# The first eight units of a two-layer model on halves of unscaled x, with the norm's row applied at eviction

## The chip, the cores and the metric

The kernel runs on one core of a Trainium2 chip. The metric is the time of one execution on the device in microseconds (us). Times are given as the median of three runs.

## The reference

The reference is a whole model in float32: a block with a state-space mixer (SSD) and a diagonal recurrence (S5), and then two layers with convolution, windowed attention and a gated feed-forward part. Only its entrance matters here: 16 meta tokens are put ahead of 512 tokens of x, and the first projection is made of the normalised result.

```python
def _rmsnorm(x, g):
    xf = x.astype(jnp.float32)
    y = xf * lax.rsqrt(jnp.mean(xf * xf, axis=-1, keepdims=True) + NORM_EPS)
    return (y * g.astype(jnp.float32)).astype(x.dtype)
...
    h = jnp.concatenate([meta, x], axis=1)            # 528 tokens x 1024
...
        n = _rmsnorm(h, g_mix[layer])
        proj = n @ w_in[layer]
        z = proj[..., :o_xbc]
        xbc = jax.nn.silu(_causal_depthwise_conv(proj[..., o_xbc:o_dt], conv_w[layer], conv_b[layer]))
        dt_raw = proj[..., o_dt:o_u]
        u = proj[..., o_u:]
        y_ssd = _ssd_mixer(xbc, dt_raw, z, ...)       # uses softplus(dt_raw + dt_bias)
        y_s5 = _s5_mixer(u, lam_re, lam_im, ...)      # uses powers of exp((lam_re + i lam_im) * step)
```

The factor of the norm is one number for each token, so it can be multiplied to a token's column of the projection after the product instead of to the input before it. The gain g belongs to a row of the weights and can't.

## The kernel before, in words

**Units.** All weight products are cut into units: 128 output features by 1024 inputs, eight tiles (kt) of 128 by 128. Products are made of two reduced-precision halves: a weight tile w becomes whi and wlo = w - whi, the activation becomes xhi and xlo, and a bank receives whi*xhi + whi*xlo + wlo*xhi. For 528 tokens a product is two matmuls of 264 columns into two banks, so a unit is 8 x 3 x 2 = 48 matmuls. There are R = 4 slots, unit g uses slot g % 4, and slot s owns the banks 2s and 2s+1. The order of units in the projection is: 0 to 7 are u (the S5 input), 8 is dt, 9 to 20 are xbc, 21 to 28 are z.

**Who does what for a unit.** The SP queue loads the raw weights (`wraw`, L2795) as soon as GpSimd has finished with the slot. ScalarE makes the high half (`split_hi`, L257), after the unit that used the slot before is done. GpSimd makes the low half (`split_lo`, L265) after that. TensorE waits for the high half and for the slot's banks to be read (`pe_unit`, L304), does the high products, waits for the low half and does the rest. The engine that reads the banks raises `acc_free`.

**Order.** Each engine's program is a list written out by hand; there is no planner. An engine does its list strictly in order. Every producer has a semaphore with a step count (`Steps`). All 86 of them are raised by four rounds at the start (`credit`), so that waits never ask for a small value. GpSimd does this in a block of its own, `setup`, with 8 more increments for `unit_done` and `acc_free`, 94 in all, and every engine meets the others at that block's end before the first DMA is issued.

**The entrance.** SP loads x in four quarters (`xin`) and then the weights of units 0 to 3. ScalarE squares the eight tiles of x (L440), VectorE adds them (L451), TensorE sums over the partitions (L528), ScalarE takes the root, VectorE the reciprocal, TensorE spreads it over the partitions as a row (L536), ScalarE copies the row to `nrs` (L459). Then, for each kt, VectorE multiplies x by gain and row into `ntt` (L580), ScalarE rounds it to xhi (L488), VectorE subtracts to xlo (L590). TensorE warms up with `keep_busy` matmuls (L509) meanwhile, then does units 0 to 3 together as the halves arrive (`pe_quad`, L338), and from unit 4 on one after the other (L304).

**Behind it.** ScalarE reads the banks of u into `uk` (L657) with a store that scatters neighbouring tokens by 66 elements, and a DMA on ScalarE's queue writes `uk` out. After the norm VectorE computes the powers for S5 (`s5_powers_dve`, small instructions of L1207, each with a drain), which need two sines of ScalarE (`s5_sin_act`, L1228 and L1229). Only then it comes to dt: it makes `dty` (L709), ScalarE takes exp and ln of it (L669, L671), and only behind those in ScalarE's list come the reads of the banks of xbc (L682, L684), each followed by the split of the unit four further on. VectorE does three taps of the convolution for each xbc tile (L724).

## Time and profile before

| | us |
|---|---|
| median of three runs | 2898.86 |
| lowest and highest | 2894.07, 2901.11 |
| the profiled execution | 2893.15 |
| its span (first to last instruction) | 2891.3 |
| TensorE busy in it | 2807.3 |
| from the span's start to the first DMA issue | 8.42 |
| to the first matmul of unit 0 | 28.58 |

The profile is of one execution. Durations and starts are read from it, in microseconds from the span's start. PE is TensorE's matmul side and PEld its weight load, DVE is VectorE, ACT ScalarE, POOL GpSimd, SP SyncE; a q behind the name is the engine's queue. L338 is line 338 of the kernel.

### The profile page before, as it was taken

To read this page: it belongs to the slowest core of one execution; us is meant where nothing else is said; L and a number is where in the kernel's file an instruction comes from. 1 tells how busy PE (TensorE), PEld (TensorE's weight loads), DVE (VectorE), ACT (ScalarE), POOL (GpSimd) and SP (SyncE) were. 2 spreads that over 40 slices of the span, in tenths; PEclk is the share of its full clock that TensorE was granted. 3 is DMA by queue.
4 is the path that set the end of the run, shared out by engine and by line. 5 is a ranking of instruction groups with operands and counts; after the bars stand their busy time and mean duration, and the time that the engine had idled before them with its cause. 6 is when DMAs were issued, how large, how long until landed. Compare 5 with 4: busy or idle time off the path is not lost.

```text
span 2891.3 us, 41476 instructions
## 1 busy us (share of the span) xinstructions
PE 2807.3 (97%) x15810; PEld 2289.6 (79%) x15810; DVE 1499.8 (52%) x1960; ACT 1083.9 (37%) x1662; POOL 1304.4 (45%) x752
## 2 busy tenths in 40 slices
PE   7998998999999999999999999999999999999998
PEld 6985744878888878877787888888887778788887
DVE  6865595453323345368874532422455877452535
ACT  4435222333323223235543422322343554342433
POOL 3444223434444264278842322222347894344343
PEclk9999999999999999999999999999999999999999
DMA  4335498333232243432232212122233223233332
GB/s 176 97 103 196 155 300 260 116 95 102 81 108 87 89 130 126 152 99 88 70 95 59 74 59 73 58 66 59 66 102 117 88 66 92 76 102 95 95 100 74
DMA packets 109736, 306.90 MB, mean 106 GB/s; under 512 B 29008, under 2 KB 37328, under 8 KB 109072
## 3 DMA queue, kind: packets, MB, share of 16 engines
q1 hardware_dynamic: 87584, 284.49, 31.2%
q10 hardware_dynamic: 19648, 16.66, 2.0%
q0 software_dynamic: 2352, 3.67, 0.4%
q8 instruction: 102, 1.67, 0.2%
q14 instruction: 50, 0.41, 0.0%
HBM read 294.95 MB, written 7.45 MB: 105 GB/s over the span
## 4 chain that ended last, share of the span: by engine, by line
PE 86%; DVE 4%; DMA 2%; POOL 2%; issue 2%; ACT 1%; DVEq 1%; SPq 0%; ACTq 0%; POOLq 0%
PE ps L304 41%; PE ps L338 17%; PE ps L329 6%; PE ps L1951 3%; PE ps L1947 3%; PE ps L1952 3%; PE ps L1955 3%; POOL wlo L265 2%; PE ps L2364 2%; PE ps L752 1%; PE ps L2024 1%; PE ps L2005 1%; DMA wada<-w_ada 1%; DVE nacc L451 1%; PE ps L1993 1%
## 5 line engine op out<-in xcount | busy, mean ns | idle before, releaser
L265 POOL TENSOR_TENSOR wlo<-wraw,whi 128x1024 fp32r<-128x1024 f32 x373 | 924.2, 2488 | 1308.4 <-ACT whi L257 1306.0
L257 ACT ACTIVATE whi<-wraw 128x1024 fp32r<-128x1024 f32 x373 | 392.0, 1054 | 454.5 <-PE ps L304 170.5
L304 PE MATMUL ps<-xah,whi 128*128 128x512 f32 x992 | 387.9, 391 | 1.7 <-issue 1.7
L304 PE MATMUL ps<-xal,whi 128*128 128x512 f32 x992 | 387.4, 391 | 0.0
L304 PE MATMUL ps<-xah,wlo 128*128 128x512 f32 x992 | 280.1, 391 | 0.0
L2250 DVE SCALAR_TENSOR_TENSOR co<-ub,vec,co 128x512 f32<-128x512 f32 (+1 forms) x216 | 254.3, 1216 | 4.2
L304 PEld LDWEIGHTS ps<-xah,whi 128*128 128x128 f32 x992 | 186.1, 188 | 42.7 <-issue 2.7
L304 PEld LDWEIGHTS ps<-xal,whi 128*128 128x128 f32 x992 | 186.1, 188 | 40.3
L304 PEld LDWEIGHTS ps<-xah,wlo 128*128 128x128 f32 x992 | 186.1, 188 | 40.2
L2351 POOL TENSOR_TENSOR co<-co,ct 128x512 f32<-128x512 f32 (+1 forms) x144 | 165.7, 1150 | 21.4 <-issue 1.3
L304 PE MATMUL ps<-hhi,whi 128*128 128x512 f32 x408 | 159.3, 390 | 0.0
L304 PE MATMUL ps<-hlo,whi 128*128 128x512 f32 x408 | 158.8, 389 | 0.0
L1113 DVE SCALAR_TENSOR_TENSOR res<-ps,mod,res 128x512 f32<-128x512 f32 (+1 forms) x64 | 47.6, 748 | 201.8 <-PE ps L329 110.0
L2707 DVE SCALAR_TENSOR_TENSOR f<-ps,vec,f 128x511 f32<-128x511 f32 x88 | 50.1, 611 | 196.3 <-ACT f L2668 196.3
L2349 POOL TENSOR_TENSOR ct<-ub,vec 128x512 f32<-128x512 f32 (+1 forms) x144 | 138.0, 958 | 26.8 <-issue 16.6
L1951 PE MATMUL ps<-xah,whi 128*128 128x512 f32 x352 | 143.5, 408 | 4.2 <-DVE ub L2262 2.6
L1952 PE MATMUL ps<-xal,whi 128*128 128x512 f32 x352 | 137.7, 391 | 0.0
L2665 ACT ACTIVATE f<-ps,vec 128x512 f32<-128x512 f32 x44 | 34.3, 780 | 186.6 <-PE ps L329 179.2
L1111 DVE TENSOR_TENSOR res<-res,ps 128x512 f32<-128x512 f32 x48 | 33.0, 688 | 132.2 <-PE ps L304 70.2
L304 PE MATMUL ps<-hhi,wlo 128*128 128x512 f32 x408 | 100.9, 389 | 0.0
L329 PE MATMUL ps<-xchi,whi 128*128 128x256 f32 x352 | 99.5, 283 | 0.0
L329 PE MATMUL ps<-xchi,wlo 128*128 128x256 f32 x352 | 99.3, 282 | 0.0
(417 smaller groups left out, 6014.8 us busy)
## 6 DMA issues: line engine op xcount, KB each, us to landing
wraw<-stream SPq DMA_DIRECT2D x425, 512.0 KB, 3.5
wada<-w_ada SPq DMA_DIRECT2D x56, 512.0 KB, 10.3
wraw<-w_ada SPq DMA_DIRECT2D x40, 512.0 KB, 3.8
biasb<-attn_bias ACTq DMA_DIRECT2D x32, 256.0 KB, 3.3
xin<-x0T SPq DMA_DIRECT2D x4, 528.0 KB, 6.5
s_u<-uk ACTq DMA_DIRECT2D x8, 264.0 KB, 2.7
res<-x0T ACTq DMA_DIRECT2D x1, 2048.0 KB, 9.1
outT<-res SPq DMA_DIRECT2D x4, 512.0 KB, 2.6
```

The source lines that it names most:

```text
L257: act.activation(whi[:, s], wraw[:, s], ACT.Copy).then_inc(hi_done[s], 1)
L265: pool.tensor_tensor(wlo[:, s], wraw[:, s], whi[:, s].bitcast(F32), ALU.subtract).then_inc(lo_done[s], 1)
L304: last = pe.matmul(ps[:, bank, 0:b - a], w[:, s, kt], x[:, kt, c0 + a:c0 + b], start=start, stop=stop)
L329: return pe.matmul(ps[:, R + s, 0:CTX], w[:, s, kt], part[:, kt], start=start, stop=stop)
L338: last = pe.matmul(ps[:, bank, 0:b - a], w[:, s, kt], x[:, kt, c0 + a:c0 + b], start=start, stop=stop)
L1947: last = pe.matmul(o, wraw[:, s, kt], x1[:, kt, 0:p.T], start=kt == 0, stop=kt == NT - 1)
L1951: pe.matmul(o, whi[:, s, kt], xah[:, kt, 0:p.T], start=kt == 0, stop=False)
L1952: pe.matmul(o, whi[:, s, kt], xal[:, kt, 0:p.T], start=False, stop=False)
L1955: last = pe.matmul(o, wlo[:, s, kt], xah[:, kt, 0:p.T], start=False, stop=kt == NT - 1)
L2250: dve.scalar_tensor_tensor(o, ub[:, m, k:k + p.T], colr(f"dw{p.l}", 1, k * 4 + m), o, ALU.mult, ALU.add)
L2349: pool.tensor_tensor(ct[:, 0:T], ub[:, m, k:k + T], colr(f"dw{l}", 1, k * 4 + m).to_broadcast([P, T]), ALU.mult)
L2351: ins = pool.tensor_tensor(o, o, ct[:, 0:T], ALU.add)
```

## The change

The first eight units work on halves of x times gain without the norm's factor (`xrh`, `xrl`), which exist as soon as x is there. ScalarE makes the high halves of x, VectorE the low ones, both in between the squares and their sum. TensorE does units 0 to 2 side by side as the halves arrive (`pe_first`), with the low products of the weights three steps late and the norm's sums and rows in the middle; banks 6 and 7, slot 3, stay with the norm. Then come unit 3 and units 4 to 7 one after the other, on the same unscaled halves. VectorE reads their banks and multiplies by the row `nrs` on the way (`u_dve`), in place of ScalarE; ScalarE only issues the DMA. The scaled halves xhi and xlo are made as before, for unit 8 and later. The `setup` block is gone: GpSimd gives 5 of the credits and the 8 increments at the start of the one block, and the other 81 credits behind its first four low halves. SP loads x and the weights in turns. `keep_busy(pe, bank, n)` was called three times, with 6, 4 and 4; now it is called once, with 4. Buffers from SC on move up to a boundary of 512 bytes (SA); their renaming is left out below.

```diff
+    xrh = at("xrh", [P, NT, TM], SA, F32R)
+    xrl = at("xrl", [P, NT, TM], SA + XB, F32R)
+    NS = SA + 2 * XB
...
+    def pe_first(pe):
+        n = NORM["mix"]
+        late = 3
+        def product(j, w, x, kt, start=False, stop=False):
+            for bank, a, b in parts_of(j, TM, True):
+                last = pe.matmul(ps[:, bank, 0:b - a], w[:, j, kt], x[:, kt, a:b], start=start, stop=stop)
+            return last
+        for kt in range(NT + late):
+            if kt < NT:
+                pe.wait_ge(raw_hi, kt + 1)
+                for j in range(R - 1):
+                    if kt == 0:
+                        hi_split(pe, U_U + j, 0, 0)
+                        pe.wait_ge(acc_free[j], 1)
+                    product(j, whi, xrh, kt, start=kt == 0)
+                pe.wait_ge(raw_lo, kt + 1)
+                for j in range(R - 1):
+                    product(j, whi, xrl, kt)
+            if kt == 6:
+                norm_sums_pe(pe, n, TM)
+            if kt == NT + late - 3:
+                norm_rows_pe(pe, n, TM)
+            if kt >= late:
+                for j in range(R - 1):
+                    if kt == late:
+                        lo_split(pe, U_U + j, 0, 0)
+                    last = product(j, wlo, xrh, kt - late, stop=kt == NT + late - 1)
+                    if kt == NT + late - 1:
+                        last.then_inc(unit_done[j], 1)
+    def u_act(act, m):
+        act.wait_ge(acc_free[slot(U_U + m)[0]], read_out(U_U + m))
+        act.dma_start(ud[m], uk[:, m % 2].rearrange("p k c -> p (k c)")).then_inc(s_uw[m % 2], 16)
+    def u_dve(dve, m):
+        s, rnd = slot(U_U + m)
+        dve.wait_ge(unit_done[s], rnd + 2)
+        if m >= 2:
+            dve.wait_ge(s_uw[m % 2], 16 * (m // 2))
+        dve.tensor_tensor(uk[:, m % 2].rearrange("p k (a c) -> p a c k", a=2),
+                          ps[:, 2 * s:2 * s + 2, 0:HALF].rearrange("p a (c k) -> p a c k", k=LB),
+                          nrs[:, :].rearrange("p (a c k) -> p a c k", a=2, k=LB), ALU.mult).then_inc(acc_free[s], 1)
+    def mix_norm_act(act):
+        for kt in range(NT):
+            norm_hi_act(act, NORM["mix"], kt, TM)
+            if kt == 2:
+                u_act(act, 0)
+                u_act(act, 1)
+                split_hi(act, U_U + R)
+            elif kt == 5:
+                u_act(act, 2)
+                split_hi(act, U_U + R + 1)
+        u_act(act, 3)
+        for m in range(2, R):
+            split_hi(act, U_U + R + m)
+    def mix_also_dve(dve, kt):
+        if kt == 1:
+            u_dve(dve, 0)
+            u_dve(dve, 1)
+        elif kt == 4:
+            u_dve(dve, 2)
+        elif kt == 7:
+            u_dve(dve, 3)
     def proj_pe(pe):
...
-        pe_quad(pe, U_U, 0, 0, xhi, xlo, TM, wide=True, **normed("mix"))
-        loop_u(U_U + R, 1, TM)
+        pe_first(pe)
+        pe.wait_ge(n_root.sem, n_root.past("root", 1))
+        pe_unit(pe, U_U + R - 1, 0, 0, xrh, xrl, TM, wide=True)
+        loop(pe, 1, lambda i: [pe_unit(pe, U_U + R + j, i, 1, xrh, xrl, TM, wide=True) for j in range(4)])
...
     def proj_act(act):
-        for m in range(NT):
-            s, rnd = slot(U_U + m)
-            act.wait_ge(unit_done[s], rnd + 2)
-            if m >= 2:
-                act.wait_ge(s_uw[m % 2], 16 * (m // 2))
-            act.activation(uk[:, m % 2].rearrange("p k (a c) -> p a c k", a=2),
-                           ps[:, 2 * s:2 * s + 2, 0:HALF].rearrange("p a (c k) -> p a c k", k=LB), ACT.Copy).then_inc(acc_free[s], 1)
+        for m in range(R, NT):
             split_hi(act, U_U + m + R)
-            act.wait_ge(acc_free[s], read_out(U_U + m))
-            act.dma_start(ud[m], uk[:, m % 2].rearrange("p k c -> p (k c)")).then_inc(s_uw[m % 2], 16)
+            u_act(act, m)
...
+        unit(4)                              # s5_powers_dve, behind its small instructions
         dve.wait_ge(s_5b, 16)
...
-        cmul(dve, bbar[:, 0], bbar[:, 1], (bin5[:, 0], bin5[:, 1]), (wide(q(CR)), wide(q(CI))), ta, tb)
+        cmul(dve, bbar[:, 0], bbar[:, 1], (bin5[:, 0], bin5[:, 1]), (wide(q(CR)), wide(q(CI))), ta, tb, lambda: unit(5))
+        unit(6)
+        unit(7)
         powers(dve, pw)
...
-    with nc.Block() as setup:
-        @setup.gpsimd
-        def _(pool):
-            for s in every_steps:
-                s.credit(pool)
-            for s in range(R):
-                pool.nop().then_inc(unit_done[s], 1)
-                pool.nop().then_inc(acc_free[s], 1)
...
-            for g in range(R):
-                load(g, g)
+            load_x(0)
+            load(0, 0)
+            load(1, 1)
+            load_x(1)
+            load(2, 2)
+            load_x(2)
+            load_x(3)
+            load(3, 3)
...
-            keep_busy(pe, 5, 6)
-            norm_sums_pe(pe, NORM["mix"], TM)
-            keep_busy(pe, 5, 4)
-            norm_rows_pe(pe, NORM["mix"], TM)
-            keep_busy(pe, 5, 4)
+            keep_busy(pe, 7, 4)
...
+            def half(kt):                    # ScalarE
+                act.wait_ge(s_in[kt // 2], 16)
+                act.activation(xrh[:, kt], xin[:, kt], ACT.Copy, scale=colr("g_mix", 1, kt)).then_inc(raw_hi, 1)
...
+            half(0)
+            split_hi(act, 0)
+            half(1)
+            split_hi(act, 1)
+            split_hi(act, 2)
+            half(2)
+            for kt in range(3, NT):
+                square(kt - 3)
+                half(kt)
+            split_hi(act, 3)
+            for kt in range(NT - 3, NT):
+                square(kt)
             root_ahead(act)
...
             for kt in range(NT):             # VectorE
+                dve.wait_ge(raw_hi, kt + 1)
+                dve.scalar_tensor_tensor(xrl[:, kt], xin[:, kt], colr("g_mix", 1, kt), xrh[:, kt].bitcast(F32), ALU.mult, ALU.subtract).then_inc(raw_lo, 1)
+                if kt >= 2:
+                    norm_add(dve, NORM["mix"], kt - 2, TM)
+            for kt in range(NT - 2, NT):
                 norm_add(dve, NORM["mix"], kt, TM)
...
+            early = [e_pa, e_pv, n_acc, n_sq, n_sum]
+            for s in early:
+                s.credit(pool)
...
             for g in range(R):
                 split_lo(pool, g)
+            for s in every_steps:
+                if s not in early:
+                    s.credit(pool)
```

## Rows read from the trace of the kernel before

**Rows 1.** The page's first part, busy time and share of the span

```profile
PE 2807.3 (97%) x15810; PEld 2289.6 (79%) x15810; DVE 1499.8 (52%) x1960; ACT 1083.9 (37%) x1662; POOL 1304.4 (45%) x752
```

**Rows 2.** The chain that ended last, 0 to 160: start, us, what

```profile
33.46 24.38 PE ps L338 x186
57.84 102.20 PE ps L304 x829
```

**Rows 3.** SP's waits to 12, its first issue (start, us), and wraw's four first loads

```profile
SPq L2772 <- PEq L2772: 7.6, 1, 7.6
...
8.42 0.40 SPq L2784 DMA_DIRECT2D pm<-s_lam  x1
...
L2795 SPq DMA_DIRECT2D wraw<-stream x4: 447/485/554, 11.0 to 12.5; - x4
...
DMA to landing us min/median/max: 8.3/9.3/10.4
```

**Rows 4.** ScalarE and VectorE by time, 81 to 141: start, us, instruction, [idle before]

```profile
81.23 1.19 ACT L657 ACTIVATE uk<-ps 128x528 f32<-128x528 f32 x1 [3.81 <-PE ps L304]
...
87.07 0.69 ACT L665 ACTIVATE dtx<-ps,vec 16x528 f32<-16x528 f32 x1 [3.79 <-PE ps L304]
...
98.14 0.64 ACT L669 ACTIVATE dty<-dty 16x528 f32<-16x528 f32 x1 [7.91 <-DVE dty L709]
...
101.85 1.04 ACT L257 ACTIVATE whi<-wraw 128x1024 fp32r<-128x1024 f32 x1
...
111.74 1.06 ACT L257 ACTIVATE whi<-wraw 128x1024 fp32r<-128x1024 f32 x1
...
103.61 36.26 DVE L724 SCALAR_TENSOR_TENSOR cac<-cin,vec,cac 128x528 f32<-128x528 f32 x24
```

**Rows 5.** ScalarE by time, 13 to 44

```profile
13.91 1.18 ACT L440 ACTIVATE nsq<-xin 128x528 f32<-128x528 f32 x2 [2.15 <-DMA xin<-x0T]
...
21.49 1.99 ACT L257 ACTIVATE whi<-wraw 128x1024 fp32r<-128x1024 f32 x2
...
25.88 0.61 ACT L459 ACTIVATE nrs<-ps 128x528 f32<-128x528 f32 x1 [0.22 <-PE ps L536]
...
42.36 1.28 ACT L1228 ACT_TABLE_LOAD   x1
```

**Rows 6.** VectorE by time; then one line's instructions: ns min/median/max, first and last start

```profile
15.19 0.71 DVE L451 TENSOR_TENSOR nacc<-nacc,nsq 128x528 f32<-128x528 f32 x1 [0.17 <-ACT nsq L440]
...
L580 DVE SCALAR_TENSOR_TENSOR ntt<-xin,vec,nrs x8: 767/769/2686, 26.5 to 40.9; 128x528 f32<-128x528 f32 x8
...
L590 DVE SCALAR_TENSOR_TENSOR xlo<-ntt,xhi x8: 699/701/2846, 30.6 to 42.4; 128x528 fp32r<-128x528 f32 x8
...
L265 POOL TENSOR_TENSOR wlo<-wraw,whi x13: 2351/2643/2860, 22.6 to 90.3; 128x1024 fp32r<-128x1024 f32 x13
```

**Rows 7.** TensorE by time, then windows: us, busy, ..., PEclk, DMA share, GB/s

```profile
20.99 1.18 PE L528 MATMUL ps<-cst,nacc 128*128 128x1 f32 x10 [1.28 <-DVE nacc L451]
...
24.15 1.70 PE L536 MATMUL ps<-cst,nst 128*128 128x128 f32 x12
...
33.46 1.43 PE L338 MATMUL ps<-xlo,whi 128*128 128x264 f32 x6 [3.90 <-DVE xlo L590]
...
33.80:37.20 3.40, 3.40 (x18) 3.40 (x17) 3.22 (x6) 1.29 (x2) 0.00 (x0) 0.50 0.51 159
```

**Rows 8.** Windows: us; busy PE, PEld, DVE, ACT, POOL; PEclk, DMA, GB/s

```profile
26.50:44.10 17.60, 12.89 (x87) 12.18 (x87) 15.80 (x16) 6.88 (x11) 6.34 (x3) 0.90 0.38 118
44.10:53.70 9.60, 9.60 (x82) 9.60 (x81) 6.95 (x36) 2.42 (x3) 0.00 (x0) 1.00 0.01 3
...
66.50:98.10 31.60, 31.60 (x262) 31.60 (x262) 26.97 (x72) 9.24 (x10) 11.84 (x5) 1.00 0.40 133
```

**Rows 9.** One line's instructions, as in the second part of rows 6

```profile
L1609 DVE SCALAR_TENSOR_TENSOR s5o<-ps,vec,sgl x8: 1145/1228/1279, 517.5 to 585.3; 128x512 f32<-128x512 f32 x8
...
L1113 DVE SCALAR_TENSOR_TENSOR res<-ps,mod,res x64: 733/750/752, 1534.1 to 2877.7; 128x512 f32<-128x512 f32 x32, 128x512 f32 x32
```

More of the change, by code:

```diff
@@ L167, in build @@
     SC = O_KC + 8 * K
+    SA = SC + (-SC) % 512
     ps = nc.alloc_psum_tensor("ps", [P, 8, 512], F32)
@@ L194, in build @@
     s_cst = sem("const_landed")
+    raw_hi, raw_lo = sem("input_hi"), sem("input_lo")
     s_more = sem("later_const_landed")
@@ L698, in proj_dve @@
     def proj_dve(dve):
-        s5_powers_dve(dve)
+        s5_powers_dve(dve, lambda m: u_dve(dve, m))
         dve.memset(xbc[:, :, 0:FRONT], 0.0)
@@ L1208, in tt, with cmul @@
         dve.drain()
-    def cmul(dve, o_re, o_im, a, b, ta, tb):
+    def cmul(dve, o_re, o_im, a, b, ta, tb, between=None):
         tt(dve, ta, a[0], b[0], ALU.mult)
@@ L1214, in cmul @@
         tt(dve, o_re, ta, tb, ALU.subtract)
+        if between:
+            between()
         tt(dve, ta, a[0], b[1], ALU.mult)
@@ L1257, in s5_param_dve, with s5_powers_dve @@
         dve.scalar_tensor_tensor(q(Q1), q(RR), -1.0, q(RR), ALU.mult, ALU.max).then_inc(e_pv.sem, 1)
-    def s5_powers_dve(dve):
+    def s5_powers_dve(dve, unit):
         dve.wait_ge(e_pa.sem, e_pa.past("sin"))
@@ L1569, in s5_act @@
         s5_hi(act, NT - 1)
-    sgl = at("sgl", [P, 2, SEQ], SC + 16 * K)
-    s5o = at("s5o", [P, NT, SEQ], SC)
+    sgl = at("sgl", [P, 2, SEQ], SA + 16 * K)
+    s5o = at("s5o", [P, NT, SEQ], SA)
     def glu_hi_pe(pe, kt):
@@ L1666, in raw_sums_ssd @@
             ssd_sums_pe(pe, c)
-    rl = at("rl", [P, 2, SEQ], SC)
+    rl = at("rl", [P, 2, SEQ], SA)
     LAST = 3
     m_v, m_h, m_l = steps("mlp_square", "v"), steps("mlp_hi", "hi"), steps("mlp_lo", "lo")
-    rv = at("rv", [P, 2, SEQ], SC + 4 * K)
+    rv = at("rv", [P, 2, SEQ], SA + 4 * K)
     def mlp_pe(pe):
@@ L1760, in mlp_dve @@
         norm_rec_dve(dve, NORM["final1"], SEQ)
-    heads = [(at(f"qT{h}", [P, SEQ], SC + 8 * K * h), at(f"kT{h}", [P, 6 * P], SC + 8 * K * h + 2 * K),
-              at(f"vT{h}", [P, 6, P], SC + 8 * K * h + 5 * K)) for h in range(4)]
+    heads = [(at(f"qT{h}", [P, SEQ], SA + 8 * K * h), at(f"kT{h}", [P, 6 * P], SA + 8 * K * h + 2 * K),
+              at(f"vT{h}", [P, 6, P], SA + 8 * K * h + 5 * K)) for h in range(4)]
     pex = at("pex", [P, 2, SEQ], O_HH)
@@ L2784, in _, with load_x @@
             sp.dma_start(pm[:, 0:3], A["s5_lam"]).then_inc(s_5in, 16)
-            for h in range(4):
+            def load_x(h):
                 sp.dma_start(xin[:, 2 * h:2 * h + 2], A["x0T"][:, 2 * h:2 * h + 2]).then_inc(s_in[h], 16)
@@ L2918, in _, with square @@
         def _(act):
+            act.dma_start(vec[:, :], A["vecs"]).then_inc(s_cst, 16)
             act.dma_start(cst[:, 0:256], A["consts"][:, 0:256]).then_inc(s_cst, 16)
-            act.dma_start(vec[:, :], A["vecs"]).then_inc(s_cst, 16)
             s5_exp_act(act)
-            for kt in range(NT):
-                norm_square(act, NORM["mix"], kt, lambda kt: xin[:, kt], TM, lambda e, kt: e.wait_ge(s_in[kt // 2], 16))
-            act.wait_ge(s_cst, 32)
+            act.wait_ge(s_cst, 32)
+            def half(kt):
+                act.wait_ge(s_in[kt // 2], 16)
+                act.activation(xrh[:, kt], xin[:, kt], ACT.Copy, scale=colr("g_mix", 1, kt)).then_inc(raw_hi, 1)
+            def square(kt):
+                norm_square(act, NORM["mix"], kt, lambda kt: xin[:, kt], TM, lambda e, kt: e.wait_ge(s_in[kt // 2], 16))
+            half(0)
[10 more added lines that the diff above has]
+                square(kt)
             root_ahead(act)
-            for g in range(2):
-                split_hi(act, g)
-            norm_act(act, NORM["mix"], TM, "eps5", between=lambda: [split_hi(act, g) for g in (2, 3)])
+            norm_act(act, NORM["mix"], TM, "eps5", split=False)
+            mix_norm_act(act)
             s5_sin_act(act)
@@ L3005, in _ @@
         def _(pool):
+            early = [e_pa, e_pv, n_acc, n_sq, n_sum]
+            for s in early:
+                s.credit(pool)
+            for s in range(R):
+                pool.nop().then_inc(unit_done[s], 1)
+                pool.nop().then_inc(acc_free[s], 1)
             for g in range(R):
                 split_lo(pool, g)
+            for s in every_steps:
+                if s not in early:
+                    s.credit(pool)
             pool_units(pool, U_U, 2)
```

46 lines of the change are left out of this document (24 added, 22 removed).

## Prediction

> **What bounds the kernel now.** I read the shares and the chain of waits first. TensorE is busy 97% of the span [rows 1]; from 33.46 us on, the chain of the first stage is TensorE alone: 24.38 us of the first four units, then 102.20 us of the next ones, with nothing between [rows 2]. So the change can act in two ways: by letting this stream begin earlier, or by breaking it later. Ahead of 33.46 the engines wait 7.6 us for the setup block, then for x, then for the norm [rows 2, 3]. The second question is what follows TensorE closely enough to stop it, and for that I went through VectorE and ScalarE up to 112 us.
>
> ScalarE reads unit 7's banks at 81.23 and those of the dt unit (unit 8) at 87.07, 5.84 us apart; units 9 to 12, the first four of xbc, then end at 92.9, 98.7, 104.6 and 110.4. Unit 13 uses slot 1, as unit 9 does: it needs unit 9's banks read and the slot's high half split. ScalarE starts those reads only when VectorE has delivered dty (98.1, after ScalarE stood 7.91 us), and the high half of unit 13 is there at 102.9, 4.8 us after dty [rows 4]. TensorE wants it at 110.4. VectorE therefore has 7.5 us to spare ahead of unit 13. That is the number this forecast turns on.
>
> **The start.** Without the setup block the DMA queues begin at about 0.75 instead of 8.42, so what hangs on x can be 7.65 us earlier: x's first quarter lands at 6.2 (13.9 before) [rows 3, 5]. Transfers land about 1.25 apart, as w0 at 11.0 + 8.3 and w3 at 12.5 + 10.4 do [rows 3]; so w0 is there at 7.8 (the first gap is longer, vecs share it), w1 at 9.0, w2 (now behind x's second quarter) at 11.55, all of x by 14.3. Only 13 of the 94 credits stay ahead of GpSimd's first low half; at 7.6/94 = 0.08 us each the other 81 take 6.5 us behind its fourth, where GpSimd has nothing to do until unit 4, and norm_root's, the only one wanted soon, is the first of them.
>
> ScalarE issues halves of x and squares at about 0.55 each, high halves of weights at 0.95 [rows 5]. It stands in order: half 2 comes behind the split of w2, at 12.5. VectorE makes a low half of x (0.70) and adds a square (0.71), 1.42 a pair with its drain (a pair of 0.77 and 0.70 comes every 1.48). Both read two SBUF tensors, and such an instruction stands while GpSimd makes a low half of weights: the slowest of L580 and of L590 took 2.69 and 2.85, where both medians are 0.77 and 0.70, and GpSimd's go on at 2.35 to 2.86 each [rows 6]. I take one VectorE instruction held up by 2.05 us for every low half that GpSimd makes. Worked through: GpSimd is busy from 8.9 to 16.9 (three halves); x's low half 2 is done at 14.6, the first add at 17.2, and ScalarE's third square waits for it. Then pairs of 1.42; the low half of x7 meets GpSimd's fourth (22.4 to 25.3) and ends at 25.8; three adds end at 28.2. TensorE issues the ten sums (1.2) and has 24 matmuls (0.1215 each, 5.84/48; 2.9) in its queue ahead of the rows (1.7) [rows 7]; ScalarE's copy takes 0.6. The norm's row is there at **34.7**, against 26.5 before: 8.2 us later, though the kernel starts 7.65 earlier.
>
> TensorE can begin when w2 is split, at 12.6, and has 18 matmuls (2.2) left behind the rows: three units end at 36.0, unit 3 at 41.8 (57.8 before). It is 16.0 us ahead there.
>
> **VectorE's chain from the norm's row to dty.** Before, it took 71.6 us, 26.5 to 98.1 (the first and the last of four stretches in [rows 8]). Twelve low halves of GpSimd held it up: 4.6 us in all over the first three instructions, nine times about 2.05 later, together 23.1. That leaves 48.5, of which 1.0 is waiting for the sine. After the change:
> - 47.5 of its own work.
> - Eight evictions of u, which were ScalarE's. The trace has no such instruction on VectorE. ScalarE's took 1.19 with this scattered store [rows 4], its copy of as many elements with a plain one 0.61 [rows 5]; VectorE's product from PSUM takes 0.75 with a plain store and 1.23 where the store steps over eight elements [rows 9]. Here the step is 66, so I take 1.25 for 528 elements, 1.17 net of overlap: 9.4. Bounds: 0.69 to 1.28; with the low one the sum is 4.1 less. They read one SBUF tensor only; of 64 plain products with a PSUM input none is over 0.752 [rows 9], so I add no hold-up.
> - The sine: ScalarE comes to it only after storing u3, splitting units 6 and 7 (1.9) and a table load with two small functions (1.7) [rows 5]: 4.4 with issue and hand-over.
> - GpSimd's low halves of units 4 to 12, without unit 6, which falls into that wait: 8 times 2.05, 16.4.
>
> Sum 77.7; from 34.7, dty comes at **112.4**.
>
> What is late next: by the same terms u4 is read at 75.2 (34.7, norm 12.0, four evictions 4.7, sine 4.4, small instructions 9.6, four hold-ups 8.2, u4 1.25, rounded). TensorE ends unit 7 at about 69.3 (41.8, four units of 5.84, and 4 us of short waits for high halves that ScalarE splits behind u1 to u3) and needs u4's banks for the dt unit. It stands 6 us, and unit 12 ends near 106.5. But unit 13 needs dty + 4.8 = 117.2, which is later still, so the first wait adds nothing. Against 110.4 that is 6.8 us late.
>
> TensorE has then stood some 10 us. After 3.9 us of standing the granted clock was at 0.50 (1.2 GHz) from 33.8 to 37.2, and 18 matmuls took twice their time, about 1.7 us more [rows 7]. I take 1.7, bounds 1.5 and 3.0 (the loss of such a stretch twice). Together **+8.5 us** at the end of unit 13.
>
> Does it stay? Behind dty come VectorE's taps, 14.3 us later than before, TensorE being 8.5 later. Their pace is 36.26/8 = 4.53 a tile against 5.84 a unit [rows 4], so these 6 us are made up in five tiles. The nearest meeting is unit 15's high half, 112.8 before, 127.1 now, where TensorE asks at about 130.6. After that all engines move together. That buffers move to a 512-byte boundary is no cost that a row shows, and fewer keep_busy matmuls lie on no path here.
>
> **Sum.** The profiled execution took 2893.15 us (span 2891.3 and 1.85 around it); with 8.5 more, 2901.65. The median of the runs is 5.7 above it, so I forecast **2907 us**. About 0.3% (8.7 us) is what a measurement of this kernel can tell from no change; the forecast lies on that edge.
>
> **Rivals.**
> 1. *VectorE's chain binds, as above*: chance 0.76, 2902 to 2913 (evictions at 0.69 take 4.1 off; a longer stretch of slow clock and a row 3 us later put 4.3 on).
> 2. *Faster: VectorE isn't the bound and TensorE keeps its lead*, 16.0 less the 4 of short waits: 2887. It takes a dty at 93.6 or before; over 0.3% faster begins at dty 96.9. For it: TensorE's 97%, and a lead that is real. Against it: after unit 7's eviction 21.0 us of small instructions follow (31.6 less five hold-ups, [rows 8]), and the change shortens none. Chance 0.07.
> 3. *Slower still: TensorE's clock stays low in the first stage*, where each step over x gives 12 to 18 matmuls with waits between. At 0.22 each the 102 matmuls up to the sums take 22.4 us from 12.6, sums at 35.0 instead of 28.2, the 24 behind them 5.3 instead of 2.9: the row, and all of VectorE's chain, 9 us later, 2916. It decides once more than 33 of the 102 run slow (3.2 us of room between 12.6 and 28.2). Against it: at 0.22 a step takes 2.6 to 4.0 us where x's halves come every 1.4 to 2.8, so TensorE would be busy without a gap, and the fall at 33.8 ended after just that [rows 7, 8]. Chance 0.08.
> 4. *No change: both waits shrink to the room there was*, with evictions at 0.69 (−4.1) and adds that miss GpSimd's fourth half (−2.3): 2901 or a little less. Chance 0.09.
>
> The trace of before has one fall of the clock near here and no loop of such steps [rows 7]. A rule of the Trainium skill speaks for the third rival: "TensorE: Matmul & The Clock Gate", section "HAM oscillation — how this bites in real kernels", has a loop whose work per step is shorter than the wait for its next operand pay the slow clock in every step. By it the sum would be 2916, by the rows 2907.
>
> **Range and chances.** 2894 to 2914 takes in case 1 whole, case 4, and the near ends of cases 2 and 3, and leaves out less than 2 in 10; it is widened below case 1 since the whole wait rests on two estimates, the row and the eviction. Slower by over 0.3% is above 2907.6: a little under half of case 1 (0.35) and case 3, 0.43. Faster: most of case 2, 0.06. Within: 0.51.
>
> **What would show it.** Right: the first half of x near 6.5; the row near 34.7; evictions of 1.2 us on VectorE; unit 3 ending near 42; TensorE standing ahead of the dt unit, and again near 107 to 117 until ScalarE's high half; dty near 112; a fall of the granted clock there. Wrong: TensorE unbroken from 42 on, evictions of 0.7, a row before 31, or a first stage at the lower clock.

## The result, and the profile after

The changed kernel takes 2909.66 us (median of 11 runs, 2903.43 to 2912.30) where the kernel before, on the same chip, takes 2894.69 us (11 runs, 2891.11 to 2903.26). The ratio is 1.0045, with a 95% interval from 1.0034 to 1.0055: 13 us slower, 9.8 to 15.9. The forecast was 2907, with a range from 2894 to 2914. It stood for 8.5 us more than a median of 2898.86; on 11 runs that median is 2894.69, so the difference came out larger than forecast (13 us, its lower bound 9.8) although the time itself is only 2.7 us off. The profiled execution took 2908.74 us, its span is 2906.6 (2891.3 before).

TensorE is busy 97% of the span, as in [rows 1], and that share tells nothing of what happened. The start went as expected, and the chain of the first stage (start, us, what) shows what came behind it:

```profile
28.20 2.00 PE ps L532 x10
30.20 5.14 PE ps L652 x24
35.35 1.45 PE ps L540 x12
37.46 0.77 DVE ntt L584
...
62.39 2.15 DVE kept L1281
65.14 2.23 DVE pm L1281
75.99 1.10 DVE uk L689
```

Where [rows 2] had TensorE alone from 33.46 us on, the chain now goes through VectorE (DVE) from the norm's row at 37.4 to dty. Three steps in it are to be looked at: 24 matmuls take 5.14 us ahead of the norm's rows, there is a hole in front of 62.39, and u4's bank is read only at 75.99.

ScalarE by time (the bracket is its idle time and what ended it) answers to [rows 4 and 5]:

```profile
36.82 0.61 ACT L463 ACTIVATE nrs<-ps 128x528 f32<-128x528 f32 x1 [6.18 <-PE ps L540]
...
113.58 0.64 ACT L743 ACTIVATE dty<-dty 16x528 f32<-16x528 f32 x1 [22.03 <-DVE dty L783]
...
117.28 1.04 ACT L259 ACTIVATE whi<-wraw 128x1024 fp32r<-128x1024 f32 x1
```

It stands 22.03 us for dty, where it stood 7.91, and splits unit 13's high half 15.4 us later than before (117.28 against 101.85). VectorE by time, and its reads of the u banks (ns min/median/max, first and last start):

```profile
62.39 2.42 DVE L1281 TENSOR_TENSOR kept<-pm 128x32 f32<-128x32 f32 x2 [4.25 <-ACT pm L1305]
64.88 2.77 DVE L1281 TENSOR_TENSOR pm<-pm 128x32 f32<-128x32 f32 x3
...
112.85 0.69 DVE L783 TENSOR_TENSOR dty<-dty,dtx 16x528 f32<-16x528 f32 x1
...
L689 DVE TENSOR_TENSOR uk<-ps,nrs x8: 1097/1152/1172, 41.1 to 86.8; 128x528 f32<-128x528 f32 x8
```

What that does to TensorE is in its waits from 36 to 200 us (us in total, times, longest), and in windows of its busy time and granted clock (us; busy; PEclk; DMA share; GB/s):

```profile
PE ps L306 <- ACT whi L259: 11.8, 4, 9.3
PE ps L306 <- DVE uk L689: 5.6, 1, 5.6
...
27.50:34.70 7.20, 6.50 (x31) 0.53 0.10 39
75.60:82.50 6.90, 5.27 (x24) 0.51 0.20 78
113.20:123.40 10.20, 5.03 (x23) 0.50 0.05 6
```

There were two long waits, 5.6 us for u4's banks and 9.3 for unit 13's high half, and three stretches at 0.50 (1.2 GHz). The clock fell each time inside a wait (at 27.9, 75.7 and 113.2). VectorE's adt copy, which opens the next stage, is at 214.9, against 204.3 before: 10.6 us late.

### The profile page after: what moved, and what is told of

It reads as the page before. It is cut to its first block, busy times and chain, and to the rows that moved or that the text cites. A ratio compares the mean times of both kernels' runs of the same rounds, so it can differ in the third digit from the quotient of the medians.

```text
span 2906.6 us, 41443 instructions
## 1 busy us (share of the span) xinstructions
PE 2811.7 (97%) x15790; PEld 2290.1 (79%) x15790; DVE 1513.7 (52%) x1976; ACT 1080.3 (37%) x1662; POOL 1302.4 (45%) x752
## 4 chain that ended last, share of the span: by engine, by line
PE 84%; DVE 6%; DMA 2%; issue 2%; DVEq 2%; POOL 2%; ACT 1%; SPq 1%; ACTq 0%; POOLq 0%
PE ps L306 39%; PE ps L340 16%; PE ps L331 6%; PE ps L2030 3%; PE ps L2026 3%; PE ps L2031 3%; PE ps L2034 2%; PE ps L2443 2%; POOL wlo L267 2%; PE ps L2103 1%; PE ps L826 1%; PE ps L2084 1%; DMA wada<-w_ada 1%; DVE nacc L455 1%; DMA wraw<-stream 1%
## 5 line engine op out<-in xcount | busy, mean ns | idle before, releaser
L331 PE MATMUL ps<-xclo,whi 128*128 128x256 f32 x352 | 99.1, 281 | 0.0
```

What stands on the lines that cost most here:

```text
L331: return pe.matmul(ps[:, R + s, 0:CTX], w[:, s, kt], part[:, kt], start=start, stop=stop)
```

## The experiments

Each kernel ran beside the kernel before. Ratios are to the latter, and 0.1% is 2.9 us. "Next stage" is the start of VectorE's adt copy in the profile.

| kernel | median us | ratio, 95% interval | dty | next stage |
|---|---|---|---|---|
| before | 2893.0 to 2896.3 | 1 | 97.4 | 204.3 |
| changed | 2909.66 | 1.0045 [1.0034, 1.0055] | 112.9 | 214.9 |
| changed, once more | 2905.82 | 1.0039 [1.0026, 1.0053] | 112.3 | 214.4 |
| e1 no block at the entry | 2885.49 | 0.9959 [0.9943, 0.9976] | 90.2 | 198.1 |
| e2 buffers moved | 2895.76 | 0.9990 [0.9977, 1.0003] | 97.5 | 204.7 |
| e12 changed, block back | 2916.45 | 1.0078 [1.0055, 1.0102] | 120.9 | 222.5 |
| e3 dty sooner | 2899.21 | 1.0008 [0.9994, 1.0022] | 100.4 | 208.8 |
| e4 sine sooner | 2908.08 | 1.0032 [1.0020, 1.0044] | 111.3 | 212.6 |
| e6 u read by ScalarE | 2902.69 | 1.0019 [1.0004, 1.0034] | 106.1 | 208.4 |
| e11 no low halves | 2894.98 | 1.0004 [0.9990, 1.0017] | 97.4 | 199.8 |
| e7 18 keep_busy | 2914.44 | 1.0063 [1.0042, 1.0084] | 115.6 | 217.7 |
| e9 4 keep_busy | 2909.63 | 1.0055 [1.0035, 1.0074] | 111.3 | 213.8 |
| e8 all repairs, 18 | 2895.99 | 1.0002 [0.9988, 1.0016] | 101.5 | 202.8 |
| e10 all repairs, 4 | 2891.52 | 0.9989 [0.9976, 1.0003] | 95.8 | 197.1 |

### Is the earlier start real? (e1, e12)

e1 is the kernel before with the setup block taken out:

```diff
-    with nc.Block() as setup:
-        @setup.gpsimd
...
         def _(pool):
+            early = [e_pa, e_pv, n_acc, n_sq, n_sum]
+            for s in early:
+                s.credit(pool)
+            for s in range(R):
+                pool.nop().then_inc(unit_done[s], 1)
+                pool.nop().then_inc(acc_free[s], 1)
+            for s in every_steps:
+                if s not in early and s is not n_root:
+                    s.credit(pool)
+            n_root.credit(pool)
             for g in range(R):
                 split_lo(pool, g)
```

> The kernel before with one part of the change alone: no block at the entry, GpSimd gives its credits inside the main block, all of them ahead of its first low half. Theory (the earlier start is real and was eaten up by VectorE's longer chain): everything from x's landing to dty moves 7.65 us earlier as a whole, VectorE keeps the 7.5 us that it had to spare ahead of unit 13, and nothing behind breaks: 7.65 us less than the kernel before, about 2887. Rival (what comes early at the entry is given back somewhere whatever is done there): no change, 2893 to 2896.

It is 0.41% faster (11.9 us, interval 7.0 to 16.5). In its profile ScalarE's copy of the row, VectorE's adt copy, and TensorE's matmuls ahead of the rows are:

```profile
14.45 3.17 PE L509 MATMUL ps<-cst 128*128 128x256 f32 x8
...
19.59 0.61 ACT L459 ACTIVATE nrs<-ps 128x528 f32<-128x528 f32 x1 [1.58 <-PE ps L536]
...
198.09 0.33 DVE L1061 COPY adt<-ps 128x160 f32<-128x160 f32 x1 [11.43 <-PE ps L838]
```

The row is 6.3 us earlier (19.59 against 25.88, [rows 5]) and so is the next stage. It isn't the whole 7.65, since the clock fell at 15.1 for 3.4 us, and the eight small matmuls took 3.17 us where they took 1.99 before. VectorE still waits 11.43 us ahead of the next stage, as before: its chain moved as a whole, and the spare time with it. The rival, that the entry's gain is given back whatever is done, falls. By the runs the gain is larger than the 6.3 us that the profile shows at the next stage (7.3 us at the end of the span); where the rest comes from is open.

e12 completes the comparison, which has each of the two parts of the change with and without the other: it is the changed kernel with the block put back and the credits taken out of the main block.

> The changed kernel with the block at the entry put back, so that only the halves of the unscaled x, the reads with the norm's row and the new order are new. Theory (the entry's gain and the loss of the rest add up, since all of the chain from x's landing over the row to dty moves as one): 6.2 to 7.65 us later than the changed kernel at dty and at the end of the projections, 2912 to 2914, 0.6 to 0.7% more than the kernel before. Rival (the start is free, since something later sets the end whatever happens at the entry): as the changed kernel, 2906.

```profile
44.19 0.61 ACT L463 ACTIVATE nrs<-ps 128x528 f32<-128x528 f32 x1 [6.00 <-PE ps L540]
...
120.86 0.70 DVE L783 TENSOR_TENSOR dty<-dty,dtx 16x528 f32<-16x528 f32 x1
```

The row is 7.4 us later than in the changed kernel, dty 8.0, the next stage 7.6. So the two parts of the change add up: in the profiles the entry is worth 6 to 8 us in either kernel, and the rest of the change costs some 17 us with the early entry (214.9 against 198.1) and 18 without it (222.5 against 204.3). By the runs the rest costs 0.78% (e12, 16 to 30 us), and the entry gives 0.41% in one kernel and 0.33 to 0.39% in the other.

### Is it VectorE's chain? (e3, e6, e11, e4)

e3 moves two small power tables, which only the phase tables behind the taps need, from ahead of dty to behind tiles 4 and 8 of the taps. They take VectorE 12.1 us (98.99 to 111.1); the 13.9 of the expectation runs on to dty itself, and the instructions from 111.1 on stay where they are.

```diff
@@ s5_powers_dve
-        dve.tensor_copy(e1[:, 0, 1], q(E8))
-        dve.tensor_copy(e1[:, 1, 1], q(E8 + 1))
-        dve.drain()
-        powers(dve, e1)
-        dve.tensor_copy(e2[:, :, 1], e1[:, :, LB])
-        dve.drain()
-        powers(dve, e2)
@@ proj_dve, loop over the tiles m
             ins.then_inc(s_conv.sem, 1)
             dve.drain()
+            if m in (4, 8):
+                s5_powers_late(dve, m // 4 - 1)
```

> The changed kernel, with the two small power tables of the state-space part (13.9 us of VectorE, 98.99 to 112.85 in the profile) moved from ahead of dty to behind the fourth-last taps they don't feed (behind tiles 4 and 8). Theory (VectorE's chain from the norm's row to dty is what stops TensorE ahead of unit 13): dty at 99.7 instead of 113.5, the high half of unit 13 at about 104.4, the wait of 11.8 us gone, and with it the stretch at the lower clock behind it (113.2 to 123.4, some 3 to 4 us): 12 to 16 us less than the changed kernel, about 2895. Rival (TensorE would be late there anyway, by its own clock and by ScalarE's splits): the wait stays above 6 us and the time above 2904.

TensorE's waits from 36 to 200, ScalarE's steps, and the next stage's first copy:

```profile
PE ps L306 <- DVE uk L689: 5.6, 1, 5.6
PE ps L306 <- ACT whi L259: 2.5, 2, 1.6
...
104.89 1.04 ACT L259 ACTIVATE whi<-wraw 128x1024 fp32r<-128x1024 f32 x1
...
208.80 0.26 DVE L1137 COPY adt<-ps 128x160 f32<-128x160 f32 x1
```

The wait of 9.3 us is gone (11.8 in total became 2.5), and so is the low clock behind it: from 82.5 to 205.4 the clock is at 1.00. TensorE's last unit of the stage is read at 200.1 instead of 212.3. So it was VectorE's chain that held TensorE up at unit 13. The time fell by some 10 us (9 to 10.7 by the ratios) and not by 12 to 16, and the next stage is only 6.1 us earlier. The last row says why: the copy has no bracket, that is no idle time ahead of it, so VectorE comes straight from its phase tables. Three of GpSimd's hold-ups, some 2 us each, fell on the moved tables, which had met none at their old place, and VectorE was 6 us late at the next stage (TensorE had been ready at about 202.7). The bound had moved to VectorE's total work.

e6 gives the eight reads of the u banks back to ScalarE, without the multiplication by the norm's row:

```diff
     def u_act(act, m):
 
+        s, rnd = slot(U_U + m)
+        act.wait_ge(unit_done[s], rnd + 2)
...
+        act.activation(uk[:, m % 2].rearrange("p k (a c) -> p a c k", a=2),
+                       ps[:, 2 * s:2 * s + 2, 0:HALF].rearrange("p a (c k) -> p a c k", k=LB), ACT.Copy).then_inc(acc_free[s], 1)
         act.wait_ge(acc_free[slot(U_U + m)[0]], read_out(U_U + m))
@@ u_dve
-        dve.tensor_tensor(uk[:, m % 2].rearrange("p k (a c) -> p a c k", a=2),
...
```

> The changed kernel, with the eight u banks read by ScalarE again, each just ahead of its store; the multiplication by the norm's row is left out of them. Theory (what the change adds to VectorE is these eight reads, 1.10 us net each, and they are paid one for one at unit 13): dty 8.8 to 9 us earlier, at 104.6, TensorE no longer stands for u4 (5.6 us), stands as long or longer ahead of unit 13, which begins 9 us earlier: about 9 us less than the changed kernel, 2900. Rival (the later row is the whole of it, the reads hide in VectorE's waits): less than 3 us.

```profile
PE ps L306 <- ACT whi L259: 13.2, 3, 11.7
```

dty comes at 106.1 (104.6 expected), 6.5 us earlier than the mean of the two profiles of the changed kernel. The wait for u4 is gone, and the wait ahead of unit 13 is longer, 11.7 us, as the theory had it. The reads were worth 8.8 us on VectorE. Of these, 3.3 came back as waits of VectorE, since ScalarE, now with the reads, delivered two of x's halves late (2.46 and 0.86 us in front of VectorE's low halves), and 0.4 by a later row; the wait for the sine was 1.5 shorter. The runs say 0.2 to 0.3% less than the changed kernel (1.0019 against 1.0039 and 1.0045), 6 to 8 us.

e11 takes away GpSimd's work beside the chain:

```diff
-            pool_units(pool, U_U, 2)
-            split_lo(pool, U_DT + R)
+            loop(pool, 2, lambda i: [split_lo(pool, U_U + j + R, i, 1, n=1) for j in range(4)])
+            split_lo(pool, U_DT + R, n=1)
```

with n=1 for 2 elements of a partition in place of 1024.

> The changed kernel, with GpSimd making only 2 elements of each partition of the low halves of units 4 to 12 instead of 1024 (the rest of those low halves is left out; TensorE's work and all signals stay). Theory (each low half holds one instruction of VectorE up by about 2.05 us, and eight of them are in the chain from the row to dty, so 16.4 us of that chain are the price of GpSimd's work beside it): dty at 96.5 instead of 112.9, u4 read at about 68 to 70 and TensorE no longer standing for it, unit 13 ready at 101.3 where TensorE comes to it at 98.5 or later: 15 to 20 us less than the changed kernel, about 2890. Rival (the long instructions of VectorE are something else, such as waits for ScalarE): dty stays above 108.

```profile
PE ps L307 <- ACT whi L259: 6.2, 1, 6.2
PE ps L307 <- DVE uk L690: 0.3, 1, 0.3
...
97.43 0.70 DVE L784 TENSOR_TENSOR dty<-dty,dtx 16x528 f32<-16x528 f32 x1
...
13.30:16.70 3.40, 3.40 (x18) 0.50 1.02 392
30.30:33.70 3.40, 3.40 (x18) 0.50 0.00 0
```

dty at 97.4, from a row at 35.4. I set the 141 instructions of VectorE between the row and dty side by side with those of the changed kernel: 133 have the same length within 0.3 us, and eight are longer in the changed kernel, by 1.78, 2.20, 1.96, 2.04, 0.97, 2.03, 2.23 and 2.23, together 15.4 us. The forecast had eight times 2.05. The chain is 14.0 us shorter, not 15.4, since one read of u now waits 1.70 us for the DMA that stores u; the other 1.4 us by which dty is earlier is the earlier row. That row is luck: no instruction of TensorE ahead of it differs from the changed kernel's, but the clock was low in other stretches, as the last two rows show (windows as above). TensorE came to unit 13 at 96.8, earlier than I had thought (98.5), since the short waits of the first units shrank too, and waited 6.2 us. The time is 2894.98, as the kernel before, 10 to 12 us less than the changed kernel and not 15 to 20, though in the profile the next stage is 15.1 us earlier.

e4 moves the sines into ScalarE's wait for the row:

```diff
-            norm_act(act, NORM["mix"], TM, "eps5", split=False)
+            norm_act(act, NORM["mix"], TM, "eps5", split=False, between=lambda: s5_sin_act(act))
             mix_norm_act(act)
-            s5_sin_act(act)
```

> The changed kernel, with ScalarE's two sines moved into its wait for the norm's row (30.6 to 36.8), ahead of the u banks' stores. Theory (the chain adds up, a wait less in it is worth its length): VectorE's wait of 4.25 us at 62.4 goes, u4 is read at about 71.8 instead of 76.0, dty comes 4.25 earlier, and so does unit 13: 4.25 us less, about 2905. Rival (the wait covered one of GpSimd's hold-ups, which now falls on an instruction): about 2.1 us less.

```profile
58.59 0.46 DVE L1281 TENSOR_TENSOR kept<-pm 128x32 f32<-128x32 f32 x2
...
60.65 2.23 DVE L1281 TENSOR_TENSOR pm<-kept,pm 128x32 f32<-128x32 f32 x1
62.95 2.29 DVE L1281 TENSOR_TENSOR pm<-pm 128x32 f32<-128x32 f32 x1
65.32 2.27 DVE L1281 TENSOR_TENSOR pm<-kept,pm 128x32 f32<-128x32 f32 x1
```

The rival was right. VectorE's wait of 4.25 us is gone, but GpSimd makes three low halves in this stretch, and all three now meet an instruction (2.23, 2.29, 2.27 instead of 0.19); with the wait there, one of them had fallen into it. u4 is read 1.6 us earlier, the next stage begins 2.3 us earlier.

### What does the clock cost? (e7, e9)

e7 and e9 put keep_busy matmuls into TensorE's wait for the last sum (25.3 to 28.2): 18 in e7, 4 in e9.

```diff
             if kt == 6:
+                keep_busy(pe, 7, 18)
                 norm_sums_pe(pe, n, TM)
```

> The changed kernel, with 18 more of the keep_busy matmuls put into TensorE's wait for the last sum (25.3 to 28.2), into a bank that nothing holds yet. Theory (this wait is what lets the clock fall at 27.87, and the slow clock doubles the 24 matmuls ahead of the norm's rows, 5.14 us instead of 2.9): no fall at 27.9, the row at about 34.6 instead of 37.4, and the whole of VectorE's chain and unit 13 with it: 2.8 us less than the changed kernel. Rival (TensorE is too little busy in this stage for the clock to stay, whatever fills one wait): the clock falls all the same and the row comes no earlier, or a little later.

TensorE and ScalarE in e7:

```profile
26.23 7.93 PE L513 MATMUL ps<-cst 128*128 128x256 f32 x36
34.00 1.08 PE L532 MATMUL ps<-cst,nacc 128*128 128x1 f32 x10
...
39.67 0.61 ACT L463 ACTIVATE nrs<-ps 128x528 f32<-128x528 f32 x1 [4.16 <-PE ps L540]
```

I had misjudged the filling: each keep_busy is two instructions of 0.22 us, 18 of them take 7.93 us, and the sums began 5.8 us late. About 1 us of that is not theirs: in this profile the clock was at 0.50 from 13.6 to 17.0 too, and they began at 26.23 where e9's began at 25.05. The row was only 2.85 late: with the clock at 1.00 the way from the sums to the row took 5.7 us instead of 8.6. That gives the price of the fall, 2.9 us (in e10, also at 1.00, the way took 5.8). Row, dty and next stage are all 2.8 us later; the runs (1.0063) can't be told from the changed kernel's.

> As the run with 18 keep_busy matmuls, with 4. There the clock stayed at 1.00 past 27.9 and the 24 matmuls ahead of the rows took 3.1 us instead of 5.1, but the 18 took 7.93 us where 1.9 were to be filled, and put the row off to 39.7. Theory (the wait ahead of the sums is what lets the clock fall, and that puts off the row): four take 1.8 us, the sums begin at 28.2 as before, the row comes at 34.5 instead of 37.4, and unit 13 as much earlier: 2.8 us less than the changed kernel. Rival (the fall comes anyway): no change.

```profile
25.05 1.89 PE L513 MATMUL ps<-cst 128*128 128x256 f32 x8
28.10 1.18 PE L532 MATMUL ps<-cst,nacc 128*128 128x1 f32 x10 [1.17 <-DVE nacc L455]
...
30.82 1.52 PE L652 MATMUL ps<-xrl,whi 128*128 128x264 f32 x6
...
35.41 0.61 ACT L463 ACTIVATE nrs<-ps 128x528 f32<-128x528 f32 x1 [5.69 <-PE ps L540]
```

With four, the wait was 1.17 us. The clock fell for half as long, at 30.7, and the row came at 35.4: 1.4 earlier than 36.8, half of what was expected, with dty 1.5 earlier. The runs don't show it (1.0055, interval 1.0035 to 1.0074, around those of the changed kernel), and the profile alone doesn't prove it: e11 has the same row, 35.4, without a filling matmul, behind a wait of 1.9 us. In e10, with the same instructions of TensorE up to here, the clock didn't fall at all between 12.6 and 37: whether it falls is not the same in every execution.

### Where the rest goes (e8, e10, e5, e2)

e8 has all repairs: e3's, e4's, 18 keep_busy, and one part of the phase tables (c = 2) made by GpSimd in the next stage:

```diff
-PHASES_DVE = 3
+PHASES_DVE = 2
@@ ssd_pool
-            if c == 2:
+            if c in (2, 3):
                 pool.wait_ge(d_ph, 1)
-                for k in range(PHASES_DVE, 4):
-                    s5_phases(pool, k)
+                s5_phases(pool, c)
```

> The changed kernel with the repairs together: the two power tables behind the taps' tiles, the sines in the wait for the row, the 18 matmuls ahead of the sums, and a third part of the phase tables made by GpSimd in the next stage in place of VectorE (which in the kernel with the tables moved was 6.1 us late at the start of the next stage, 208.8 instead of 202.7, with no wait left from 107 on). Theory (VectorE's work between the row and the next stage is the bound of this kernel; it loses 9.8 of phases, 2 of the wait for the sine and begins 2.8 sooner): the next stage begins at about 197, as early as in the kernel with only the entry's block gone (198.1), 2885 to 2888. Rival (another engine binds by then, or GpSimd's extra part delays the next stage): 2893 or more.

The next stage began at 202.8, not at 197, since the row came at 39.5 and not at 34.6 (the 18 matmuls again). e10 is e8 with 4:

> The kernel with all repairs, with 4 keep_busy matmuls instead of 18. There the next stage began at 202.8 and VectorE was almost without a wait from the row (39.5) on. Theory (VectorE's work from the row on sets the start of the next stage): row at 34.5, next stage at 197.8, 5 us less than that kernel, about 2891. Rival (TensorE, 200.2 at its last unit there, has waits of its own and gives only part): 2893 to 2896.

```profile
33.82 0.61 ACT L463 ACTIVATE nrs<-ps 128x528 f32<-128x528 f32 x1 [2.39 <-PE ps L540]
...
197.11 0.32 DVE L1137 COPY adt<-ps 128x160 f32<-128x160 f32 x1 [1.11 <-PE ps L915]
```

Row 5.7 earlier, next stage 5.7 earlier: the theory's step holds, and VectorE is again almost without a wait (1.11 us). It opens the next stage 1.0 us ahead of e1, though its TensorE is at work on the first three units from 12.3 on, where e1's begins the first four at 23.2: the whole lead of TensorE is worth only that, as VectorE has to follow. The runs give 2891.5 (0.9989), less than half of the 7.2 us that the next stage is early against the kernel before. In the profile 3.2 of the 7.2 are gone by 520 us and 1.4 more by 665, which wasn't looked into, and 3.1 between 1500 and 2506 us, in the stages of the moved buffers (see e2 below). e1, the block alone, stays the fastest.

e5 is the changed kernel once more:

> The changed kernel once more, as the yardstick for the runs beside it and for how much two executions of one kernel differ. Theory: the end of the projections is again 10 to 11 us later than in the kernel before, and what lies behind it differs by some us either way, since the lower clock in the next stage is not in the same place every time. Rival (the 4.8 us behind the projections belong to the change): the profiled execution is 15 us later again and the later stages show the same steps.

Its next stage is at 214.4 (214.9 in the first profile), its span 2902.3 against 2906.6, so single profiles differ by 4 us behind the projections. e2 is the kernel before with only the addresses changed:

```diff
     SC = O_KC + 8 * K
+    SA = SC + (-SC) % 512
...
-    h2lo = at("h2lo", [P, 8, SEQ + CTX], SC, F32R)
-    xchi = at("xchi", [P, NT, CTX], O_KC, F32R)
+    h2lo = at("h2lo", [P, 8, SEQ + CTX], SA, F32R)
+    xchi = at("xchi", [P, NT, CTX], SA - 8 * K, F32R)
```

> The kernel before with another part alone: the buffers behind the context's move to a 512-byte boundary, as the change moves them, and nothing else. In the profiles the changed kernel is 10.5 us late at the end of the projections and 15.3 us late at its end. Theory (this move costs nothing; what is late behind the projections is the spread between executions): within 2 us of the kernel before. Rival (the moved buffers cost the other 4.8 us, in the stages that use them): 4 to 5 us more than the kernel before, about 2899.5.

By the runs it costs nothing, 0.9990 [0.9977, 1.0003]. Its profile is 10.8 us longer all the same, and TensorE's windows from 200 us on show the larger part of the reason: 0.62 granted, with the clock low for 34.1 us in one piece (13.7 and 10.2 in the kernel before), 7 us lost by 336 us. Such a stretch is in e4's profile too, at 0.64, and in neither of the two of the changed kernel.

```profile
200.00:245.00 45.00, 39.43 (x200) 0.62 0.18 61
245.00:345.00 100.00, 92.59 (x626) 0.95 0.63 216
```

But one thing repeats. Between 1666 and 2194 us (times of the kernel before, read at ScalarE's splits) all twelve profiles with moved buffers lose 3.9 to 4.3 us, and between 2443 and 2506 they win 1.3 back; e1 does neither. These are TensorE's groups from 1749 to 2149, busy us and mean ns, first in e1 (old addresses), then in e2 (moved):

```profile
L304 PE MATMUL ps<-xal,whi 128*128 128x512 f32 x224 | 88.4, 395 | 0.0
L304 PE MATMUL ps<-xah,whi 128*128 128x512 f32 x224 | 87.7, 391 | 0.0
L304 PE MATMUL ps<-xah,wlo 128*128 128x512 f32 x224 | 80.2, 394 | 0.0
```

```profile
L305 PE MATMUL ps<-xal,whi 128*128 128x512 f32 x224 | 89.4, 399 | 0.0
L305 PE MATMUL ps<-xah,whi 128*128 128x512 f32 x224 | 89.2, 398 | 0.0
L305 PE MATMUL ps<-xah,wlo 128*128 128x512 f32 x224 | 80.6, 399 | 0.0
```

The three groups together are busy 259.2 us instead of 256.3. The changed kernel has 398 and 399 as well, the kernel before 391 to 394; in the profiles of e5, e9, e10 and e12 the mean is 398 to 399 too. The four tensors that these matmuls read (xah, xal, whi, wlo) were not moved.

## Why the forecast was right, and what it missed

**The mechanism** was right, the number partly by luck. The forecast difference, 8.5 us, lies below the measured interval (9.8 to 15.9); the time is only 2.7 us off since the three runs it was added to had a median 4.2 us above that of the 11. And of its three outcomes the forecast gave most to the one within 0.3% (0.51) and 0.43 to the one that came, slower by over 0.3%.

**The start**: right. x's first half at 6.48 us (6.5 forecast), the adds' end at 28.14 (28.2).

**The row**: forecast 34.7, measured 37.4. The step "TensorE issues the ten sums (1.2) and has 24 matmuls (… 2.9) in its queue" took the full clock. They took 2.00 and 5.14, as the clock had fallen at 27.9 in the wait of 2.9 us for the last sum; e7 shows the price, 2.9 us. The range allowed for a row 3 us later, the sum didn't. Unit 3 ended at 45.0, mostly for the same reason (41.8 forecast), 12.8 us ahead of before and not 16.0.

**VectorE's chain**: forecast 77.7, measured 76.1 (37.4 to 113.5). The eight reads took 1.10 to 1.17, not 1.25; the wait for the sine was 4.25 (4.4), the hold-ups 15.4 (16.4). e6, e4 and e11 removed the causes of the three, one each. dty was there at 113.5 (112.4): two errors, of the row (2.7 late) and of the chain (1.6 short), that partly cancelled. The 21.0 us of small instructions behind unit 7's eviction are 21.35 by the terms given for them; they took 25.6, of which two hold-ups are 4.5.

**Unit 13**: its high half at 118.3 (117.2), 7.9 us behind the 110.4 of before; I had 6.8. Its first matmul began at 118.38 instead of 110.20, 8.2 later. Behind it the clock was low until 123.4, and the unit's first 32 matmuls took 6.26 us instead of 3.89 (118.38 to 124.64; before, 110.20 to 114.09): 2.4 us, where I took 1.7 (bounds 1.5 to 3.0). Together 10.6, which is what the next stage is late. The forecast had 8.5: the terms that were mis-sized are the way to the row, of which 1.1 us is left at unit 13's high half, and the clock (0.7); 0.3 more is the step from unit 12's end (110.4) to the start of unit 13 (110.2), which overlapped before. e3 shows that the wait at unit 13 is the one that binds. The earlier wait, for u4's banks, had a stretch of low clock behind it too (75.7 to 82.5), which the sum didn't name; like that wait it cost nothing, as TensorE had to wait for unit 13 anyway.

**"It stays"**: right. At the next stage VectorE has 11.4 us to spare in the kernel before and still 11.4 in the changed one; e3 and e10 use it up. I had not asked how much VectorE had left, and that is why repairs of the order give less than their length.

**"Buffers move … is no cost that a row shows"**: the rows of one stage show about 3 us, and 2.4 to 3.1 are left at 2506 us. Whether the kernel's time has them is open. Over the eleven profiles of the changed kernel and its variants, the time (by its ratio, of 2895 us) lies on average 2.8 us above what the start of the next stage gives; e2's runs, with an upper bound of 0.9 us, speak against it. By the same figure e1, with the old addresses, lies 5.7 us below, so the figure is no surer than that. The runs of one kernel mostly spread over 8 to 18 us, and the profiles differ most in how long the clock is low between 200 and 345 us, so no more can be told from them. What in the moved addresses makes those matmuls slower wasn't tried.

**The rivals.** The first one bound. *Faster, VectorE isn't the bound* fell with ScalarE's wait of 22.03 us. *No change* fell: the evictions were at 1.15, not 0.69. *The clock low in the first stage*: from 12.5 to 25.3 TensorE ran at 1.00, with 0.4 us of waits in all; the steps followed each other without the gaps that the rival needed. Until the next stage the clock fell three times, each time in one long wait. But three of the variants' profiles (e7, e8, e11), with the same instructions of TensorE so far, had the clock at 0.50 for 3.4 us from 13.2 to 13.6 on, in the middle of this loop. There TensorE had stood 1.7 to 2.0 us ahead of 12.6, for w2's high half, against 1.2 to 1.7 in the other profiles; whether that is the reason wasn't tried. It stayed within the 3.2 us of room that the rival counts: in e11 the sums still began at 28.14. So the rival fell by its size, and not because the clock can't fall there. The rule of the Trainium skill that stood for it ("TensorE: Matmul & The Clock Gate", section "HAM oscillation — how this bites in real kernels") asks for steps with less work than wait; here a step had 0.7 us of work for each group of six matmuls and no wait, so neither the changed kernel's trace nor those three, with one slow stretch each and not one in every step, speak against the rule: this loop wasn't a case of it.

## What to carry to other kernels

Before giving an engine's early start to a busy TensorE, count the work of the engine that follows it from the same event on, up to the next stage; if that event comes later, the lead is worth no more than that engine's spare time (TensorE was 13 us ahead at the end of unit 3, and with all repairs 1 us was left against e1 at the next stage, and nothing by the runs, 0.9989 against 0.9959). Separate the parts of such a change: the block at the entry alone gives 0.41%, and the rest took more than that away. A wait taken out of a chain that runs beside GpSimd returns less than its length, and matmuls that are to hold the clock must be counted by their own duration in a row.

## What the runs showed of the hardware

- A low half on GpSimd (2.4 to 2.9 us, two SBUF inputs) held up one VectorE instruction with two SBUF inputs, by 1.8 to 2.3 us in seven cases of eight (0.97 in the other), however short it is (0.19 becomes 2.23); without it, eight such hold-ups, 15.4 us, are gone (e11). The u reads, with one input in SBUF and one in PSUM, weren't held up: one of the eight lies inside a low half of GpSimd (79.47, 1.15 us, and the same read in eight more profiles), and none in any profile took over 1.21. The Trainium skill, "SBUF — State Buffer", section "SBUF: two separate sides", says that the two engines lock a pair of ports against each other for a whole instruction, VectorE's with two SBUF inputs among them; the trace agrees.
- VectorE's product from PSUM with a store that steps over 66 elements took 1.10 to 1.17 us for 528 elements in the changed kernel, ScalarE's copy of the same form 1.14 to 1.17 (e6).
- TensorE's matmuls of one stage were 1 to 2% slower (398 to 399 against 391 to 395 ns) when buffers elsewhere in SBUF, not their own, were moved by less than 512 bytes, with the same instructions at full clock. The cause is open.
- The granted clock isn't the same in every execution. After a wait of 1.2 us for the last sum it fell in one profile (e9, for 3.4 us) and not in the other with the same instructions of TensorE (e10). With the same instructions of TensorE up to there it was at 0.50 for 3.4 us inside the first stage in e7, e8 and e11, and at 1.00 in the changed kernel's two profiles. Between 200 and 245 us it was 0.62 in e2, 0.64 in e4, 0.73 in the kernel before and 0.85 in the changed kernel, whose stages begin up to 11 us apart.
